# Turning the next head one query block sooner, and moving the residual scaling on GpSimd in a two-block transformer kernel

## What is computed

```
h = rms_norm(x, norm_g);  p = h @ w_in            # c_q, c_kv, k_pe, z_a, u_f, z_f, gates
q = rms_norm(c_q) @ w_uq;  k, v = rms_norm(c_kv) @ w_ukv      # 8 heads, 64+32 wide
q, k = rope(rms_norm(q)), rope(rms_norm(k))
o_a = softmax(q k^T * scale) v                    # 8 heads x 4 query blocks of 128
m = sigmoid(..) * ((o_a*silu(z_a)) @ w_attn_proj) + sigmoid(..) * ((fft2(u_f)*silu(z_f)) @ w_fourier_proj)
x = x + m @ w_out
```

## Time and profile before

| | |
|---|---|
| median of three runs | 1554.18 us (1552.07 to 1554.40) |
| profiled execution | 1555.09 us, of which the core's span 1553.3 us |
| PE busy | 1505.9 us, 97% of the span |
| DVE, ACT, POOL busy | 835.5, 610.5, 369.8 us |
| PE's share of the chain that ended last | 84% (DVE 10%, ACT 3%) |
| block 2 | from about 755 us to the end; its two attentions 879 to 954 us and 1271 to 1346 us |

### The profile page before, as it was taken

How to read it: one execution, slowest core, us unless ns; L and a number is a source line. 1 busy time by engine, 2 the same in 40 slices (tenths; PEclk the granted TensorE clock), 3 DMA queues, 4 the chain that set the end, 5 groups by cost and what they waited for, 6 DMA issues and landing times.

```text
span 1553.3 us, 19030 instructions
## 1 busy us (share of the span) xinstructions
PE 1505.9 (97%) x7248; PEld 1249.0 (80%) x7248; DVE 835.5 (54%) x1330; ACT 610.5 (39%) x927; POOL 369.8 (24%) x354
## 2 busy tenths in 40 slices
PE   5999999999999999999999999999999989999998
PEld 4887788888888888888887788888888778888886
DVE  5536764344543434334579685443447878644445
ACT  3325772324331313224334565333333456532332
POOL 2004560001100000001368243110115824321011
PEclk8999999999999999999999999999999999999999
DMA  5421003332233232322232002323223200233321
GB/s 144 126 82 54 23 17 106 109 108 93 82 108 109 81 108 82 107 97 92 76 95 81 1 1 82 109 81 108 86 84 108 82 0 1 72 103 97 92 99 55
DMA packets 136449, 125.99 MB, mean 81 GB/s; under 512 B 21808, under 2 KB 131632, under 8 KB 136368
## 3 DMA queue, kind: packets, MB, share of 16 engines
q1 hardware_dynamic: 135183, 124.83, 25.7%
q10 hardware_dynamic: 1184, 0.07, 0.1%
HBM read 122.75 MB, written 2.39 MB: 81 GB/s over the span
## 4 chain that ended last, share of the span: by engine, by line
PE 84%; DVE 10%; ACT 3%; issue 2%; DMA 1%; POOL 0%; ACTq 0%; DVEq 0%
PE G L1678 66%; PE S L1660 5%; PE G L1781 5%; PE G L1660 3%; PE T L1762 3%; DVE w L1142 2%; PE G L1843 2%; ACT w L865 1%; DVE ab L1160 1%; DVE sq L1284 1%; DVE hs L1566 1%; DVE v L1156 1%; DMA gains<-in_norm_mix 1%; DVE sq L1540 0%; ACT ab L915 0%
## 5 line engine op out<-in xcount | busy, mean ns | idle before, releaser
L1678 PE MATMUL G<-gx,w 128*128 128x512 f32 x3024 | 696.1, 391 | 3.3 <-DVE w L1142 3.3
L1678 PEld LDWEIGHTS G<-gx,w 128*128 128x128 f32 x3024 | 567.8, 188 | 124.3 <-DVE w L1142 4.2
L1142 DVE TENSOR_TENSOR w<-raw,w 128x2048 fp32r<-128x2048 f32 x112 | 262.0, 2339 | 221.7 <-ACT w L865 221.6
L865 ACT ACTIVATE w<-raw 128x2048 fp32r<-128x2048 f32 x112 | 211.6, 1890 | 139.3 <-PE G L1678 110.1
L1678 PE MATMUL G<-kvb,w 128*128 128x512 f32 x960 | 218.4, 389 | 0.0
L1678 PEld LDWEIGHTS G<-kvb,w 128*128 128x128 f32 x960 | 180.2, 188 | 37.4
L716 POOL TENSOR_TENSOR t<-t,rden 128x512 f32<-128x512 f32 (+2 forms) x128 | 109.7, 857 | 155.5 <-DVE rden L1290 155.4
L748 POOL TENSOR_TENSOR t<-sig 128x512 f32<-128x512 f32 x24 | 35.3, 1472 | 357.6 <-DVE sig L1357 357.6
L1413 DVE TENSOR_TENSOR x<-G,x 128x512 f32<-128x512 f32 x56 | 38.6, 689 | 115.4 <-PE G L1678 115.4
L927 ACT ACTIVATE t<-sq,nm 128x512 f32<-128x512 f32 (+3 forms) x128 | 80.1, 626 | 29.5 <-DVE nm L1284 29.2
L810 POOL TENSOR_TENSOR sumsq_f<-sumsq_f,sq_f 128x512 f32<-128x512 f32 x7 | 9.1, 1300 | 333.4 <-ACT sq_f L895 333.4
(11 more groups left out here) (210 smaller groups left out, 1844.9 us busy)
## 6 DMA issues: line engine op xcount, KB each, us to landing
raw<-in_w_in SPq DMA_DIRECT2D x98, 512.0 KB
raw<-in_w_up SPq DMA_DIRECT2D x32, 512.0 KB
raw<-in_w_down SPq DMA_DIRECT2D x32, 512.0 KB
raw<-in_w_out SPq DMA_DIRECT2D x24, 512.0 KB
raw<-in_w_attn_proj SPq DMA_DIRECT2D x8, 512.0 KB
raw<-in_w_fourier_proj SPq DMA_DIRECT2D x8, 512.0 KB
xin<-in_x SPq DMA_DIRECT2D x2, 1024.0 KB, 6.6
raw<-in_w_proj_a SPq DMA_DIRECT2D x8, 256.0 KB
```

The costliest lines, as they stand in the source:

```text
L865: nc.scalar.activation(K.w[:, j % 2, 0, 0:n], K.raw[:, j % 2, 0:n], ACT.Copy).then_inc(K.w_hi, 1)
L1142: nc.vector.tensor_tensor(K.w[:, s, 1, 0:n], K.raw[:, s, 0:n], K.w[:, s, 0, 0:n].bitcast(F32), ALU.subtract).then_inc(K.w_lo, 1)
L1678: mm = nc.tensor.matmul(b[:, :], w(p, k), x(q, k), start=(k == i == 0), stop=(k == kts - 1 and i == len(PASSES) - 1))
```

## The change

1. `turned(n)` names a head one block sooner: head h is turned by PE after block 4(h-2)+2 (before: +3), and `qk_hi(h)` and `qk_lo(h)` stand ahead of block 4(h-2)+3 in ACT's and DVE's loops (before: 4(h-2)+4). In both layers.
2. The sixteen scalings of x leave the latent stage. In the first layer POOL does them inside the attention, one after the probabilities of each even block (`scaled_x`): eight by the gain (blocks 0 to 14), then eight by the factor (16 to 30). In the second layer they are gone.
3. The second layer takes its statistics by the plain `stat`; its prior, its spreading matmul on PE and the two `memset` of ones are gone.
4. The factor is kept in `sumsq`, which is free in that time; for that `rotate` works in place (still six operations of the same sizes).

```diff
-        h = n // TT + 1
-        return h if self.kind == "L" and n % TT == 0 and 2 <= h < HEADS else None
+        h = n // TT + 2
+        return h if self.kind == "L" and n % TT == TT - 1 and h < HEADS else None
...
+            if A.kind == "L" and A.layer == 0 and n % 2 == 0:
+                scaled_x(n // 2)
...
+    def scaled_x(i):
+        k = i % KT
+        if i < KT:
+            nc.gpsimd.tensor_tensor(K.x[:, k, :], K.x[:, k, :], K.gains[:, 2, k:k + 1].broadcast_to([P, SEQ]),
+                                    ALU.mult).then_inc(K.x_fin, 1)
+        else:
+            pool.wait_ge(K.prior_taken, 1)
+            pool.wait_ge(K.x_fin, k + 1)
+            nc.gpsimd.tensor_tensor(K.x[:, k, :], K.x[:, k, :], K.sumsq[:, :], ALU.mult).then_inc(K.x_fin, 1)
...
-        nc.gpsimd.tensor_tensor(rc, x1, sin, ALU.mult).then_inc(K.rope_ok, 1)
+        nc.gpsimd.tensor_tensor(x1, x1, cos, ALU.mult).then_inc(K.rope_ok, 1)
...
-        pool.wait_ge(K.prior_taken, Num(1, (l, 1)).value())
-        pool.wait_ge(K.tile_out, Num(G_L + 5, (l, GL)).value())
-        for k in range(KT):
-            nc.gpsimd.tensor_tensor(K.x[:, k, :], K.x[:, k, :], K.gains[:, 2, k:k + 1].broadcast_to([P, SEQ]),
-                                    ALU.mult).then_inc(K.x_fin, 1)
-        for k in range(KT):
-            pool.wait_ge(K.x_fin, Num(k + 1, (l, 2 * KT)).value())
-            nc.gpsimd.tensor_tensor(K.x[:, k, :], K.x[:, k, :], K.rstd_f[:, :], ALU.mult).then_inc(K.x_fin, 1)
...
+        if l:
+            stat(norm, s, meanwhile)
+            spread(s)
+            return
...
-        nc.vector.memset(K.prior[:, :], 1.0).then_inc(K.prior_ok, 1)
-        dve.wait_ge(K.prior_full, Num(1, (l, 1)).value())
-        nc.vector.tensor_copy(K.rstd_f[:, :], K.T[1][:, :]).then_inc(K.prior_taken, 1)
+        dve.wait_ge(K.prior_full, 1)
+        nc.vector.tensor_copy(K.sumsq[:, :], K.T[1][:, :]).then_inc(K.prior_taken, 1)
...
-            if k == (1 if l == 0 else 0):
+            if k == 1 and l == 0:
                 pe.wait_ge(K.prior_diag, Num(1, (l, 1)).value())
                 nc.tensor.matmul(K.T[1][:, :], K.ones[:, :], K.sq[:, 1, :], start=True, stop=True).then_inc(K.prior_full, 1)
```

More of the change, by code:

```diff
@@ L256, in allocate @@
     K.ab = at("ab", 40, [P, 2, 2, TT, SCOL], F32R)
-    K.rstd_f = at("rstd_f", 40, [P, SEQ], F32)
     K.qkh = K.ab[:, :, :, :, :].rearrange("p r h t s -> p (r h t s)").rearrange(
@@ L768, in rotate @@
         sin = K.rope[:, ts, half:ROPE].unsqueeze(2).broadcast_to([P, 2, HEADS, half])
-        ra, rb, rc = [b.rearrange("p (t h c) -> p t h c", t=2, h=HEADS)
-                      for b in (K.rt[:, 0, :], K.rt[:, 1, :], K.sumsq[:, 0:2 * P])]
+        ra, rb = [K.rt[:, i, :].rearrange("p (t h c) -> p t h c", t=2, h=HEADS) for i in range(2)]
         r = Num(12 * q + 6 * i, (l, 24))
@@ L774, in rotate @@
             pool.wait_ge(K.rope_ok, r.value())
-        nc.gpsimd.tensor_tensor(ra, x1, cos, ALU.mult).then_inc(K.rope_ok, 1)
+        nc.gpsimd.tensor_tensor(ra, x1, sin, ALU.mult).then_inc(K.rope_ok, 1)
         nc.gpsimd.tensor_tensor(rb, x2, sin, ALU.mult).then_inc(K.rope_ok, 1)
-        nc.gpsimd.tensor_tensor(rc, x1, sin, ALU.mult).then_inc(K.rope_ok, 1)
+        nc.gpsimd.tensor_tensor(x1, x1, cos, ALU.mult).then_inc(K.rope_ok, 1)
         nc.gpsimd.tensor_tensor(x2, x2, cos, ALU.mult).then_inc(K.rope_ok, 1)
         pool.wait_ge(K.rope_ok, (r + 4).value())
-        nc.gpsimd.tensor_tensor(x1, ra, rb, ALU.subtract).then_inc(K.rope_ok, 1)
-        nc.gpsimd.tensor_tensor(x2, x2, rc, ALU.add).then_inc(K.rope_ok, 1)
+        nc.gpsimd.tensor_tensor(x1, x1, rb, ALU.subtract).then_inc(K.rope_ok, 1)
+        nc.gpsimd.tensor_tensor(x2, x2, ra, ALU.add).then_inc(K.rope_ok, 1)
     def silu_f(l, t):
@@ L1047, in program_act @@
         split(j + 1, f)
-        act.wait_ge(K.prior_ok, Num(3, (l, 4)).value())
+        if l == 0:
+            act.wait_ge(K.prior_ok, 3)
+        else:
+            act.wait_ge(K.s_taken, (s + 1).value())
         nc.scalar.activation(K.d4[:, :], K.v4[:, :], ACT.Sqrt).then_inc(K.stat_sqrt, 1)
@@ L1194, in rsqrt, with stat @@
         dve.wait_ge(sem, (n + 4).value())
-    def stat(norm, s):
+    def stat(norm, s, meanwhile=None):
         dve.wait_ge(K.s_full, (s + 1).value())
         nc.vector.tensor_scalar(K.v4[:, :], K.S[s % 2][:, 0:TT], 1.0 / D, EPS, ALU.mult, ALU.add).then_inc(K.s_taken, 1)
+        if meanwhile is not None:
+            meanwhile()
         dve.wait_ge(K.stat_sqrt, (norm + 1).value())
@@ L1638, in program_vector @@
                   Num(KT + 2 * i, (l, KT)), sig_num(l, 8 + 4 * i), i, (lambda: za_lo(HALF - 1)) if i == 0 else None)
-        dve.wait_ge(K.x_fin, Num(2 * KT, (l, 2 * KT)).value())
-        nc.vector.memset(K.gains[:, 2, :], 1.0).then_inc(K.gain_ok, 1)
+        if l == 0:
+            dve.wait_ge(K.x_fin, 2 * KT)
         for i in range(4):
```

## The result

The changed kernel takes 1545.63 us (median of six runs, 1542.15 to 1548.37) where the kernel before took 1554.29 beside it (six runs). The ratio of the two is 0.9937, with a 95% interval of 0.9922 to 0.9952, or 7.5 to 12.1 us less. The profiled execution took 1545.05 us, with a span of 1543.3 us; PE is busy in 1502.0 us of it, DVE in 823.3, ACT in 608.2, POOL in 339.1.

What follows compares the result with a forecast made beforehand. PE, 97% busy, was taken as the bound, stalling 8.1 us for `ab` in block 2. First layer 4.65 plus second 6.16 gave 10.8 us off 1555.09, 1544.3, less 0.9 for the median: 1543.4 us, range 1537.5 to 1548.5.

Steps and rivals of the forecast that it cites:

- Part 1: Attention, heads turned one block sooner: the stall for `ab` goes, DVE's loop becomes the bound; gain 3.3 us a layer.
- Part 2: POOL's scalings inside the first attention: cost only at its last transposes, 0.75 us (0.65 to 0.85).
- Part 3: Latent stage without the scaling: DVE's splits no longer contend with POOL; gain 2.1 us a layer, 4.2 in both.
- Part 4: Second layer's start, from sums to spreading matmul, without the T matmul between: gain 0.76 us.
- C: Rival: latent stage gives back its gain, since DVE is late there for other reasons; 1547.6 us, chance 0.2.
- B: Rival: the whole stall goes and PE sets the pace in attention; 1538.8 us, chance 0.15.
- E: Rival: attention gains nothing, since `qk_lo`, behind `out` and `low`, comes no sooner; 1550.0 us, chance 0.07.
- F: Rival: POOL's scalings fall into DVE's attention loop, each at full cost, 20 us; 1563 us, chance 0.03.
- D: Rival: the clock in the Fourier stage falls not at all, 1541.6 us, or, second form, in both layers, 1545.2; chance 0.1.

Runs made afterwards that it cites:

- combined: Changed kernel with out_later's edit, dummy products in PE's Fourier-stage waits, and POOL's last scaling of x behind the last probabilities; 1537.41 us, 0.9877 of the kernel before.
- out_later: Changed kernel with DVE's copy of a finished head (`out`) one query block later, behind `qk_lo`; 1543.30 us, 0.9915 of the kernel before.
- scale_only: Changed kernel with the old rule of `turned`, so everything but the turn; first attention 75.47 us, second 74.80, latent stages 70.52 and 70.39.
- scale_after: Changed kernel with POOL's sixteen scalings of x all behind the first attention; first attention 72.11 us, the stage behind it 203.47.
- turn_only: Kernel before with only the new rule of `turned`, one block sooner; attentions 72.12 and 71.77 us, latent stages 73.01 and 73.48.
- wait_more: Changed kernel with one more DVE reduction ahead of each of the last two z tiles, lengthening PE's waits; Fourier stages 18.63 and 18.64 us.

## Why the prediction was right, and where its terms were not

**The bound and the sign.** Right: PE's standing still in block 2 was the place, and what was won there stayed won: 201.31 us in each kernel of the table and in combined.

**Part 1, the turn.** Forecast 3.3 us a layer, with DVE's loop as the new bound. The mechanism is right: no wait for `ab`, no idle time ahead of `qk_lo`, a wait for `nm` (0.26 us on average in the turned heads, 0.27 forecast), and an even head lasts 8.53 us to the digit. The mis-sized term is `out` at 0.60 us, taken from an even head for all. For odd heads it costs 0.25 us more, twice within the five heads, and the step at block 19 takes 0.34 more: 0.84 us in all, and blocks 7 and 27 are 43.49 us apart instead of 42.65. The trace of before had the row; an odd head on DVE:

```profile
1299.47 0.69 DVE L1298 COPY z<-G 64x512 f32<-64x512 f32 x1
1300.20 0.69 DVE L1310 TENSOR_TENSOR pt_l<-T,pt_l 128x512 fp32r<-128x512 f32 x1
```

0.73 us from the one to the other where the earlier trace rows have 0.60. It cost nothing then, since each head lasted 9.19 us by the stall, whichever it was; as soon as DVE's loop is the bound, it counts. The stages gained 2.69 in the second layer, and 2.34 + 0.52 = 2.86 in the first without POOL's part. The 8.26 us for PE alone was too much as well, since out_later runs an even head in 8.07. I had subtracted only the stall for `ab` from the head's length.

**Part 2, POOL.** Forecast 0.75 (0.65 to 0.85), measured 0.52 in scale_only and 0.50 in scale_after, below the range, and all at the last transposes as said. The wait there is 1.27 us where I expected about 1.4. The multiply of the probabilities stayed at 1.04 us, and DVE wasn't slowed by the two-tensor scaling.

**Part 3, the latent stage.** Forecast 2.1 a layer, measured 2.76 and 2.45. The path is the one described: splits at 2.29, no wait at the q tiles, DVE waiting for PE at the second u tile, no wait left at the last z tiles. Two terms were small. PE's gain by the first z and u product was 1.04 us and not 0.7: beside the wait of 0.47 the pace of late evictions cost 0.5 where I had estimated 0.2. And v's low part alone takes 0.41 us; I had taken 0.53 from a pair that still stood half beside POOL, so DVE was earlier than I thought and the whole wait of 1.84 us went, not 1.4 of it. The first layer's 2.76 is less sure than the second's 2.45: its stage of before had the clock's fall behind that wait, and turn_only, with the same code there and no fall, took 73.01 instead of 73.31.

**Part 4.** 0.84 us measured, 0.76 forecast, in both scale_only and the changed kernel.

**The sum.** 10.8 us forecast for these stages, 11.1 measured: 1.1 us more in the latent stages and the start, 0.2 more from POOL, 1.1 less from the turn. The sum is better than its terms, and that is luck. Luck has a part in the whole times too: the two profiled spans differ by 10.0 us since 2.7 lost in the Fourier stages, 4.1 won in block 1 and 2.5 lost at the end come to little together. The medians are 8.7 us apart.

**The rivals.** C falls: nothing is given back. B falls for this kernel, but out_later shows what it spoke of, since a rest of the stall was to be had behind DVE's copy. E and F fall with the rows above. D happened in its second form: in the profiled execution the clock fell in both layers, and the two stages took 0.3 and 2.3 us more than before. What part of the 2.2 us between 1543.4 and the median of 1545.6 this is can't be said, since of the other executions only the mean granted clock is known (0.989 to 0.995 over the six, the highest in the shortest of them, 1542.15 us) and untouched code moved by 4.1 and 2.5 us. The Trainium skill's rule in D (TensorE: Matmul & The Clock Gate, Part 1), that activity releases the throttle, agrees with the dummy products, beside which the clock fell in 0 of 6 stages; the change alone left the three waits in a row, and the clock fell in both layers.

## What to carry to other kernels

When a stall goes, walk the next engine's loop instruction by instruction, and do it for each kind of turn of the loop: here even and odd heads differ by 0.25 us that the old stall had hidden. Then ask which instruction in the heaviest step needn't stand there; moving a copy by one block gave 2.2 us more per attention, nearly as much as the turn itself (2.8 and 3.0). Where PE stands still for a microsecond several times in a row and its clock then falls, products of no use in those waits are worth 1.4 to 2.4 us each time.

## What the runs showed of the hardware

- DVE and POOL together: a split of 128x2048 takes 3.05 us instead of 2.29 beside POOL's multiply of x, also where POOL's second operand is a broadcast column; a 128x256 subtract of two SBUF operands takes 0.72 instead of 0.41. DVE's attention work, with one operand in PSUM, isn't slowed at all beside sixteen such multiplies.
- A DVE copy that reads and writes partitions 64 to 127, where its neighbours start at 0, costs 0.11 us ahead of it and some 0.13 behind it, 0.25 in all.
- PE's clock fell in the Fourier stage in 9 of 16 unfilled stages of eight like kernels, with single waits of 0.3 to 1.4 us, so one profile doesn't tell whether a fall belongs to a kernel. In wait_more it fell in both.
- Untouched code up to layer 1 took 756.96 to 763.15 us over all profiles, in the order of the granted clock from 129 to 147 us (1.00 to 0.62), and the stretch from the last attention to the end 207.3 to 209.8. A part worth under 3 us has to be read from its stage.
